# One hybrid layer on one core: half of the scale columns moved from VectorE to TensorE, the entry of the expert stage reordered, and the last sums dealt anew

## The reference

```
mod = c_act @ ada_w + ada_b                     # six rows of 1024: sh1, sc1, g1, sh2, sc2, g2
u = rmsnorm(h, norm1_g) * (1 + sc1) + sh1
h = h + g1 * mixer(u)                           # RG-LRU branch and gated linear attention
u = rmsnorm(h, norm2_g) * (1 + sc2) + sh2
h = h + g2 * moe(u)                             # 8 of 128 experts per token, and a shared one
out = rmsnorm(h, final_g)
```

## Time and profile before

| | us |
|---|---|
| median of 3 runs | 1233.4 (1233.11 to 1236.43) |
| the profiled execution | 1233.88 |
| its span | 1232.1 |
| TensorE busy | 1192.7 (97%) |
| VectorE busy | 690.8 (56%) |
| ScalarE busy | 541.3 (44%) |
| GpSimd busy | 222.4 (18%) |
| `lr` starts / products of `("v", 0)` start | 40.73 / 48.67 |
| `gate_up(0)` / `gate_up(1)` start | 596.37 / 604.92 |
| last store of SyncE issued | about 1229 |

### The profile page before, as it was taken

The page is one execution under the profiler, slowest core; times in us unless marked ns, Lnnn a source line. Parts: engine busy times, 40 slices in busy tenths (PEclk is TensorE's granted clock), DMA queues, the critical chain, the costliest instruction groups (busy, mean ns, idle before and its releaser), DMA issues.

```text
span 1232.1 us, 20837 instructions
## 1 busy us (share of the span) xinstructions
PE 1192.7 (97%) x5729; PEld 703.4 (57%) x5730; DVE 690.8 (56%) x1281; ACT 541.3 (44%) x630; POOL 222.4 (18%) x323
## 2 busy tenths in 40 slices
PE   5899999999999999998999999999999999999996
PEld 5687887777888888884444343443434434344342
DVE  4542347586572676867545454454545546555567
ACT  5572224745422413231435454454544546566521
POOL 1000000000000000003332332333323234343300
PEclk9799999999999999999999999999999999999999
DMA  9633503353495485655798889888888888999796
GB/s 342 209 107 115 187 5 103 103 200 126 153 343 186 141 276 197 222 198 240 291 354 326 319 321 340 309 335 314 308 339 301 329 307 326 382 403 417 279 417 268
DMA packets 88593, 321.56 MB, mean 261 GB/s; under 512 B 13040, under 2 KB 16344, under 8 KB 66152
## 3 DMA queue, kind: packets, MB, share of 16 engines
q1 hardware_dynamic: 69192, 279.69, 61.5%
q0 software_dynamic: 14432, 32.85, 7.0%
q10 hardware_dynamic: 4928, 8.49, 2.0%
HBM read 292.35 MB, written 48.24 MB: 276 GB/s over the span
## 4 chain that ended last, share of the span: by engine, by line
PE 90%; DVE 4%; DMA 3%; ACT 2%; SPq 1%; issue 1%; DVEq 0%; ACTq 0%
PE psum L1713 33%; PE psum L1947 28%; PE psum L1957 14%; PE psum L1936 4%; DMA w_now<-expert_rows 2%; PE psum L1686 2%; PE psum L1815 1%; PE psum L1986 1%; PE psum L1746 1%; DMA ring<-in_ada_w 1%; PE psum L1775 1%; PE psum L1804 1%; PE psum L1871 1%; PE psum L1727 1%; PE psum L1863 1%
## 5 line engine op out<-in xcount | busy, mean ns | idle before, releaser
L1947 PE MATMUL psum<-w_now,xT 128*64 128x512 f32 x1568 | 347.3, 595 | 0.0
L1947 PEld LDWEIGHTS psum<-w_now,xT 128*64 128x64 f32 x1568 | 108.2, 137 | 197.2 <-issue 195.9
L1957 PE MATMUL psum<-w_now,mask 128*64 128x512 f32 x784 | 176.6, 592 | 0.0
L1020 ACT ACTIVATE w_now<-stage 128x2048 f32 x79 | 147.7, 1906 | 37.2 <-issue 33.6
L482 DVE TENSOR_TENSOR w_lo<-ring,w_hi 128x1024 fp32r<-128x1024 f32 x80 | 94.7, 1222 | 86.0 <-ACT w_hi L475 84.0
L747 POOL COPY w_now<-stage 128x1024 f32 x79 | 82.0, 1055 | 335.5 <-PE psum L1957 314.6
L1713 PE MATMUL psum<-uT_hi,w_hi 128*128 128x512 f32 x352 | 139.3, 396 | 1.1 <-DVE w_lo L482 1.1
L1713 PE MATMUL psum<-uT_hi,w_lo 128*128 128x512 f32 x352 | 137.0, 389 | 0.0
L1713 PE MATMUL psum<-uT_lo,w_hi 128*128 128x512 f32 x352 | 136.9, 389 | 0.0
L475 ACT ACTIVATE w_hi<-ring 128x1024 fp32r<-128x1024 f32 x80 | 82.7, 1056 | 122.1 <-PE psum L1713 59.5
L1531 DVE COPY w_now<-stage 128x2048 f32 x79 | 95.5, 1242 | 45.7 <-issue 42.0
(11 more groups left out here) (361 smaller groups left out, 1666.4 us busy)
## 6 DMA issues: line engine op xcount, KB each, us to landing
stage<-in_exp_w_gu SPq DMA_DIRECT2D x106, 1024.0 KB, 8.4
stage<-in_exp_w_down SPq DMA_DIRECT2D x53, 1024.0 KB, 5.9
ring<-in_w_in SPq DMA_DIRECT2D x56, 512.0 KB, 5.5
expert_rows<-zero_fill SPq DMA_DIRECT2D x16, 1024.0 KB, 8.2
ring<-in_ada_w SPq DMA_DIRECT2D x32, 512.0 KB, 5.0
stage<-expert_rows SPq DMA_DIRECT2D x12, 1024.0 KB, 18.8
ring<-in_ada_w SPq DMA_DIRECT2D x4, 1024.0 KB, 13.4
scale_w<-in_ada_w SPq DMA_DIRECT2D x4, 1024.0 KB, 14.7
```

Of the source, the lines that this page charges most:

```text
L1020: act.activation(w_now[:, q, 2:4], staged(turns[q] + STAGES - 1, 2, 2), ACT.Copy).then_inc(gu_moved[1], 1)
L1947: mm = pe.matmul(moe_bank(GU)[at, :], xT[:, s % 2, k, at], gu_part(q, k), start=(k == 0), stop=(k == KT - 1))
L1957: mm = pe.matmul(moe_bank(Y0 + g)[at, :], hT[:, j, at], dn_part(q, j, g), start=(j == 0), stop=(j == 1))
```

## The change

There are three parts.

1. Head. The second scale block (`("scale", 1)`) is no longer summed by VectorE. TensorE takes it raw: one product with zeros and then 32 products of one column. VectorE now writes all eight full copies (`u_whole`), and ScalarE none. `wlr_lo` stands behind `scale_cols(1)` and `u_whole(4..7)` on VectorE. GpSimd waits for `("scale", 1)` before it clears the place of `wlr_lo`.
2. Entry of the expert stage. On TensorE `turn_rows(0)` comes ahead of `find(2)`, `gate_up(0)` ahead of `find(3)`, and `turn_rows(1)` behind `gate_up(0)` and five shared products. VectorE does `move_first(0)` ahead of `find_rows(2)`. ScalarE does `move_second(0)` ahead of `rows_turned(0)`, and `rows_turned(1)` behind the first `silu`.
3. End. Rank 6 of tiles 0 and 1 goes from TensorE to VectorE. For the last tile TensorE adds ranks 0 to 2 (before 4 to 6), VectorE ranks 3 to 5 in `add_slots` and 6 and 7 behind (before 0 to 3, and 7), and the load groups of the last tile are (0,3), (3,4), (4,6), (6,8).

```
-        rank_groups = [...] * (TT - 1) + [((0, 2), (2, 4), (4, 7), (7, 8))]
+        rank_groups = [...] * (TT - 1) + [((0, 3), (3, 4), (4, 6), (6, 8))]
+        pe_ranks = (4, 5), (4, 5), (4, 5, 6), (0, 1, 2)
+        dve_ranks = (0, 1, 2, 3, 6), (0, 1, 2, 3, 6), (0, 1, 2, 3), (3, 4, 5)
+        late_ranks = (7,), (7,), (7,), (6, 7)
...
-            pool.wait_ge(row_sum, 3)
+            pool.wait_ge(row_sum, 2)
+            wait_job(pool, ("scale", 1))
             pool.memset(wlr_lo.bitcast(F32), 0.0).then_inc(lr_zero, 1)
...
-            sum_rows(scale_w[:, 1], scale_in[1], tmpT[:, 1], range(4))
...
             scale_cols(0)
-            sum_rows(scale_w[:, 1], scale_in[1], tmpT[:, 1], range(4, KT))
-            for k in range(4):
+            u_whole(range(4))
+            for k in range(2):
                 u_lo(k)
+            scale_cols(1)
+            for k in range(2, 4):
+                u_lo(k)
+            u_whole(range(4, KT))
             dve.wait_ge(lr_split, 1)
             dve.wait_ge(lr_zero, 1)
             tt(wlr_lo[:, :, :, 0:RANK], wlr_four, ...).then_inc(lr_split, 1)
-            scale_cols(1)
-            for k in (6, 7):
-                ...
...
-            columns(("scale", 1), 3, tmpT[:, 1])
+            start_job(("scale", 1))
+            pe.matmul(bank(("scale", 1))[:, 0:4], ident[:], zeros[:, 0:4], start=True, stop=False)
+            for k in range(KT):
+                pe.wait_ge(scale_in[1][k // 4], 16)
+                for j in range(4):
+                    mm = pe.matmul(bank(("scale", 1))[:, j:j + 1], scale_w[:, 1, k, j * P:(j + 1) * P], c_col[:, k:k + 1], ...)
+            end_job(mm)
...
+            act.wait_ge(tables_ready, 1)
+            move_second(0)
             rows_turned(0, 0)
-            act.wait_ge(tables_ready, 1)
             shared_gate(1)
-            move_second(0)
+            silu(0)
             rows_turned(1, 1)
-            silu(0)
...
-                for r in (4, 5, 6):
+                for r in pe_ranks[t]:
```

More of the change, by code:

```diff
@@ L492, in rows_of, with group_of @@
             return row_buffers[s % UNROLL]
+        def group_of(t, r):
+            return [r < end for first, end in rank_groups[t]].index(True)
         def ranks_of(t, first, n=1):
@@ L1567, in _ @@
             pick_rows(2)
-            shared_up(0)
+            move_first(0)
             find_rows(2, 2)
             pick_rows(3)
-            move_first(0)
+            shared_up(0)
             find_rows(3, 3)
             pick_rows(AHEAD)
+            gated_up(0)
             shared_up(1)
-            gated_up(0)
             move_first(1)
@@ L1635, in rank, with slot_in @@
                 return ranks_of(t, r).rearrange("p o d -> p (o d)")
+            def slot_in(t, r):
+                dve.wait_ge(slots_in[t][group_of(t, r)], 16)
             def add(t, part):
-                own(tt(rank(t, 0), rank(t, 0), part, ALU.add))
+                acc = rank(t, dve_ranks[t][0])
+                own(tt(acc, acc, part, ALU.add))
                 own.settle()
             def add_slots(t):
[L1644 to L1648, removed]
+                slot_in(t, dve_ranks[t][0])
+                for r in dve_ranks[t][1:]:
+                    slot_in(t, r)
+                    add(t, rank(t, r))
             def add_rest(t):
@@ L1654, in add_rest @@
                 dve.wait_ge(h_in[t], 16)
-                own(tt(h_back[t], h_back[t], rank(t, 0), ALU.add))
+                own(tt(h_back[t], h_back[t], rank(t, dve_ranks[t][0]), ALU.add))
                 own.settle()
-                dve.wait_ge(slots_in[t][3], 16)
-                tt(h_back[t], h_back[t], rank(t, 7), ALU.add).then_inc(h2_res, 1)
+                for r in late_ranks[t]:
+                    slot_in(t, r)
+                    last = tt(h_back[t], h_back[t], rank(t, r), ALU.add)
+                    if r < TOP_K - 1:
+                        own(last)
+                        own.settle()
+                last.then_inc(h2_res, 1)
             dve.wait_ge(fg_in, 16)
@@ L1768, in _ @@
             columns(("scale", 0), 2, tmpT[:, 0])
-            columns(("scale", 1), 3, tmpT[:, 1])
+            start_job(("scale", 1))
[3 more added lines that the diff above has]
+                for j in range(4):
+                    mm = pe.matmul(bank(("scale", 1))[:, j:j + 1], scale_w[:, 1, k, j * P:(j + 1) * P], c_col[:, k:k + 1], start=False, stop=(k == KT - 1 and j == 3))
+            end_job(mm)
             pe.wait_ge(lr_split, 2)
@@ L1964, in _ @@
             shared_products(4)
-            find(2)
-            shared_products(1)
             wait_emptied(pe, "bstart_row")
             turn_rows(0, 0, 16)
+            find(2)
             shared_products(2)
-            find(3)
-            shared_products(4)
-            turn_rows(1, 1, 16)
             pe.wait_ge(tables_ready, 1)
@@ L1975, in _ @@
             gate_up(0, 0, pe.value_load(copies_thru[0:1, 0:1], min_val=1, max_val=TABLE))
+            find(3)
+            shared_products(5)
+            turn_rows(1, 1, 16)
             wait_emptied(pe, ("sgu", 1))
```

20 lines of the change are left out of this document (8 added, 12 removed).

## The result

The changed kernel takes 1254.99 us (median of 3 runs, 1254.28 to 1255.62) against 1233.4. The ratio is 1.0164, with a 95% interval of 1.0142 to 1.0187. It is slower, as forecast, but by more: the profiled span grew from 1232.1 to 1253.3 us, 21.2 where the sum said 14.4. The time lies above the range.

What follows compares the result with a forecast made beforehand. TensorE, busy 97% of the span, was taken as the bound, with VectorE's tail behind it. 10.9 + 1.3 + 2.2 = 14.4 us on 1233.88 gave 1248.3, forecast as 1247.8; 8-in-10 range 1239 to 1250.5.

Steps and rivals of the forecast that it cites:

- What bounds it: Whole kernel: TensorE is busy 97% of the span, so delaying the first product of ("v", 0) delays everything behind it.
- Head, +10.9: Before the dense products: 64 one-column matmuls at 0.218, then 4.5 us of VectorE work, start lr at 51.6, against 40.73.
- Entry, +1.3: Expert stage's start: gate_up(0) comes 5.4 us earlier, but turn_rows(2) waits for ScalarE's 1.02 copy and starts 1.3 later.
- Entry, the first gather: Expert stage's start: the gather issued at 581.15 lands 7.0 later, at 588.15, so TensorE's idle of 1.40 stays.
- Clock behind gaps: Before the dense products: after TensorE's idle from 47.1 to 51.6, lr starts at the low clock and takes 7.94 us.
- End, +2.2: Last tile: ranks 4 and 5 land later and VectorE adds four sums, not three, ending at 1231.3 against 1229.1.
- Mixer, 0: From the first product of ("v", 0) to find(0): no change in length, 0 us.
- Fast columns: Rival for the start: the one-column products run at 2.4 GHz, +4.1 there, 1241.0 in all; chance 0.17.
- vanished columns: Rival for the start: the one-column products leave the path, sum +1.7, 1235.1; chance 0.08, shared with later slack absorbing costs.
- entry and end pay: Rival: early gate_up(0) removes idle (only 1.40) and the last tile lands earlier (tail 1.5 at most); no chance of its own.
- Range: Whole kernel's time: 8 in 10 between 1239 and 1250.5 us.

Runs made afterwards that it cites:

- The head alone: The kernel before with only the change's first part, the second scale block summed by TensorE's one-column products: ratio 1.0085.
- The wide form of the same sums: The kernel before with only the change's first part, its 32 one-column products turned into 8 products of 512 columns: ratio 1.0066.
- the mended entry: The kernel before with only the change's second part, TensorE's two last waits for shared products' banks moved behind the loop's first gate_up: ratio 1.0020.
- the entry alone: The kernel before with only the change's second part, turn_rows(0) and gate_up(0) moved ahead: ratio 1.0051.
- the mended kernel: The whole change against the kernel before, with wlr_lo earlier, the two bank waits inside the loop, and the last tile's sums reordered: ratio 1.0074.

## Why the prediction was right and wrong

- **What bounds it.** Right. The head alone put 10.3 to 11.9 us on the start of the dense products and 10.5 on the time.
- **Head, +10.9.** Right: +10.1. The price of 0.218 a matmul was measured as 0.215, `lr` was forecast at 51.6 and started at 51.12, `("v", 0)` at 59.6 and 58.77. Of the two prices that the earlier trace rows showed, the choice rested on what the same product did at 12.83: it kept the slow pace to its end. The wide form of the same sums shows that this is the products' form, not the place. The Trainium skill (TensorE: Matmul & The Clock Gate, "LDWEIGHTS (loading the stationary operand)"), whose rule would have had the job done near 40, is not borne out where the clock is low: 0.215 each here.
- **Entry, +1.3: this step failed.** It measured 7.5 (6.05 and 1.4 behind it). The text said that `turn_rows(2)` "waits for ScalarE's 1.02 copy", with bounds of +0.2 and +2.6. I had summed the work of the engines and their waits, and the way into the loop is neither: TensorE's sequencer needs about 3.4 us from VectorE's release to the first matmul, and before it did so under `gate_up(0)`. By moving `gate_up(0)` ahead, the change took that cover away; the prediction named covers only for ScalarE's copy. Against the mended entry, which costs 1.9 and has the forecast wait, the changed kernel shows 2.1 more at this gap, 1.2 for shared products and 0.2 for small ones at the low level, 0.6 more idle for the gather, and 1.4 for `gate_up(1)` at the low level: with the 1.9 that is 7.4.
- **Entry, the first gather.** Off by a little: I said that the idle stays at 1.40, and it was 2.22, since the gather landed 7.66 us after its issue, not 7.0, and was issued later against the shared products. In the runs with the entry's part it was 1.63 to 2.32.
- **Clock behind gaps.** I had allowed for it in the head only. Where the low level followed a gap at the entry, it cost 1.2 us more behind 2.22 us and 1.6 behind 3.24 in the changed kernel, and 2.6 behind 3.34 in the entry alone. It did not follow every gap (not 1.63 and 1.80 us, nor 2.32 in the mended kernel). What decides this is open.
- **End, +2.2.** Right in its steps: TensorE without a wait, VectorE held by ranks 4 and 5, then without idle. The size, +1.95 in the changed kernel and +2.18 alone, holds against the profile that the forecast started from. I had not seen that TensorE's idle of 2.19 is mostly followed by sums at the low level. Against such an end the part costs 0.3 to 0.8 only.
- **Mixer, 0.** It showed +1.6, and by the other profiles this is scatter.
- **Rivals.** Fast columns are out by 0.215 a matmul, vanished columns too. That entry and end pay is out for the change as it stands, but the end does pay once its order is changed (0.9980): I had bounded what the tail could win by 1.5, VectorE's idle before it adds TensorE's last sums. With the new order it won 2.0, since these sums themselves end earlier.
- **Range.** The upper end held only the bounds of the three terms as I saw them, 2.7 us up. An unseen fourth cost had no room in it. It also started from an execution near the fast end of the scatter: 14.4 on the later median of 1236.6 gives 1251.0, an estimate, and 1254.99 is 4.0 above that. The changed kernel did not run beside those executions.

## What to carry to other kernels

Before you move a long job away from the entry of a loop, ask what it was covering on its engine's own sequencer. Register loads and branches are not in the busy time and not in the waits: they show as "issue", and only once nothing is queued ahead of them; here two waits, moved behind the loop's first `gate_up`, took the entry's ratio from 1.0051 to 1.0020. When a late landing stands ahead of ready work in an in-order engine, change the order before you judge the split of the work: the two orders of one split lie 4.2 us apart in the profiles (54.56 and 50.34 from the last expert product to VectorE's end), and 1.0011 and 0.9980 in the ratios.

## What the runs showed of the hardware

One-column fp32 matmuls with 128 x 128 weights cost 0.215 to 0.234 us at a granted 0.50 and 0.116 at the high level, and 64 of them in a row, 13.8 us without a break, left the clock at the low level. Products of 512 columns in the same place brought the high level within some 4 us of their start (35.8 to 39.5). At the entry, idle gaps of 2.22 and 3.24 us in the changed kernel and of 3.34 us in the entry alone were followed by stretches of about 3 to 7 us at the low level; `gate_up(1)`, behind the two longer ones, took 8.49 and 8.70 us instead of 7.09. A gap of 2.32 us in the mended kernel was not. At the old end idles of 1.94 to 2.17 us were followed by last sums at the low level in six profiles (7.07 to 7.11 us), and idles of 1.98 and 2.19 us by sums at the high level in two (5.42 us): the length of the gap alone does not decide. An earlier start of `lr` by 2 us brought the dense products forward by 0 to 1.5 us, and the time did not show it.
